# An expert stage on one Trainium2 core: low halves of the weights on GpSimd alone, gating and sparse sums in PSUM

## What is computed

```python
s1, i1 = lax.top_k(s[:, :, 0], K); s2, i2 = lax.top_k(s[:, :, 1], K)
sc, ci = lax.top_k(cand, K)                 # 16 experts for each of 8 heads
idx = e1 * PEER_NKEYS + e2; g = softmax(sc)
a = einsum('cd,chkd->chk', xc, u[ic])       # up, for the chosen rows of u
act = gelu(a) * gc
out = einsum('chk,chkd->cd', act, v[ic])    # down
```

## Time and profile before

| | us |
|---|---|
| median of 3 runs | 4909.03 (4905.62 to 4913.11) |
| the profiled execution | 4913.5 |
| its span | 4911.7 |
| busy over the whole span: TensorE, VectorE, ScalarE, GpSimd | 4389.7, 2406.8, 2512.6, 1767.7 |

### The profile page before, as it was taken

One profiled execution on the slowest core, in us unless ns is written; L12 is line 12 of the kernel. 1 busy time (PEld: TensorE's weight loads), 2 busy tenths in 40 slices (PEclk: granted clock), 3 DMA queues, 4 the chain that ended last, 5 costly groups with the idle time before them and its releaser, 6 DMA issues.

```text
span 4911.7 us, 66130 instructions
## 1 busy us (share of the span) xinstructions
PE 4389.7 (89%) x24326; PEld 2291.1 (47%) x24326; DVE 2406.8 (49%) x4548; ACT 2512.6 (51%) x3525; POOL 1767.7 (36%) x910
## 2 busy tenths in 40 slices
PE   3889999989999988997989999998897888887888
PEld 2454444544444434443444444455454554454554
DVE  4554220434334334424421022354599996796894
ACT  2457544547544445744567444364465544445444
POOL 1134433024433334443034333210342127629437
PEclk9889989999999999998899998897999999999999
DMA  3246322017322223622022322200234467768766
GB/s 145 90 152 253 105 80 82 1 50 263 128 85 85 70 70 135 252 95 69 22 73 98 100 90 82 82 31 1 75 120 133 135 185 257 252 194 281 228 199 233
DMA packets 160502, 623.60 MB, mean 127 GB/s; under 512 B 17824, under 2 KB 17952, under 8 KB 156816
## 3 DMA queue, kind: packets, MB, share of 16 engines
q1 hardware_dynamic: 123120, 483.65, 28.6%
q0 software_dynamic: 37152, 136.80, 8.8%
HBM read 618.29 MB, written 2.10 MB: 126 GB/s over the span
## 4 chain that ended last, share of the span: by engine, by line
PE 52%; DVE 19%; issue 14%; POOL 10%; ACT 3%; DMA 1%; SPq 0%; POOLq 0%; DVEq 0%; ACTq 0%
PE ps L720 13%; PE ps L722 13%; PE ps L721 13%; POOL halves L550 6%; POOL rows L606 3%; DVE halves L2550 2%; DVE rows L2512 2%; PE ps L771 2%; DVE rows L2571 1%; DVE rows L2520 1%; DVE lasting L2531 1%; DVE rows L2376 1%; PE ps L916 1%; DVE rows L2541 1%; PE ps L906 1%
## 5 line engine op out<-in xcount | busy, mean ns | idle before, releaser
L550 POOL TENSOR_TENSOR halves<-ring,halves 128x1024 f16<-128x1024 f32 x592 | 1330.2, 2248 | 2473.5 <-ACT halves L1355 2471.3
L720 PE MATMUL ps<-h,halves 128*128 128x512 f16 (+1 forms) x2912 | 1062.7, 365 | 110.5 <-POOL halves L550 72.0
L721 PE MATMUL ps<-h,halves 128*128 128x512 f16 (+1 forms) x2912 | 1061.5, 365 | 0.0
L722 PE MATMUL ps<-h,halves 128*128 128x512 f16 (+1 forms) x2912 | 1060.5, 364 | 0.0
L720 PE MATMUL ps<-rows,halves 128*128 128x512 f16 (+2 forms) x2544 | 914.8, 360 | 91.4 <-DVE rows L1948 44.0
L1352 ACT ACTIVATE ring<-ring 128x1024 f32<-128x1024 f32 x718 | 752.9, 1049 | 439.8 <-DMA ring<-wstream 436.0
L721 PE MATMUL ps<-rows,halves 128*128 128x512 f16 (+2 forms) x2544 | 913.6, 359 | 0.0
L722 PE MATMUL ps<-rows,halves 128*128 128x512 f16 (+2 forms) x2544 | 913.1, 359 | 0.0
L1355 ACT ACTIVATE halves<-ring 128x1024 f16<-128x1024 f32 x718 | 758.8, 1057 | 22.8
L720 PEld LDWEIGHTS ps<-h,halves 128*128 128x128 f16 x2912 | 287.2, 99 | 437.6 <-POOL halves L550 89.6
L722 PEld LDWEIGHTS ps<-h,halves 128*128 128x128 f16 x2912 | 287.6, 99 | 297.0 <-issue 13.5
(11 more groups left out here) (269 smaller groups left out, 5284.5 us busy)
## 6 DMA issues: line engine op xcount, KB each, us to landing
ring<-wstream SPq DMA_DIRECT2D x718, 512.0 KB
rows<-ada SPq DMA_DIRECT2D x96, 768.0 KB, 4.8
rows<-ada_first SPq DMA_DIRECT2D x24, 1024.0 KB, 5.9
x<-x_in POOLq DMA_DIRECT2D x1, 2048.0 KB, 14.0
rows<-u_rows,h POOLq DMA_INDIRECT x128
rows<-v_rows,h POOLq DMA_INDIRECT x128
out<-x SPq DMA_DIRECT2D x8, 256.0 KB, 3.9
rows<-phase_nsa SPq DMA_DIRECT2D x1, 1600.0 KB, 6.9
```

The costliest lines, as they stand in the source:

```text
L550: nc.gpsimd.tensor_tensor(halves[:, j % RING, 1, :], ring[:, j % RING, :], halves[:, j % RING, 0, :], ALU.subtract).then_inc(s_wlow, 1)
L720: nc.tensor.matmul(out_, high, act16[:, 0, :], start=first, stop=False)
L721: nc.tensor.matmul(out_, high, act16[:, 1, :], start=False, stop=False)
L722: return nc.tensor.matmul(out_, low, act16[:, 0, :], start=False, stop=last)
```

## The change

- All low halves are subtracted by GpSimd, in the same place of its queue as before; VectorE's `weights_low` is gone. ScalarE splits three slots ahead (SPLIT_AHEAD) in this stage, and first waits until TensorE has used the slot that the halves' buffer held. SP's loads of this stage wait for the low half (`s_wlow`) of the slot whose ring buffer they overwrite.
- `gated` becomes a view of PSUM banks 6 and 7: `gate` works in place where TensorE wrote. A spread then waits for the low half of the block two before (`s_actl`). Both batches of a block are spread together.
- `sparse_in` is copied by ScalarE into PSUM banks 2 and 3 before stretch 0, the steps work on that, and ScalarE copies the sum back before TensorE folds it. The up products of these stretches are left two banks, 0 and 1.
- VectorE's queue goes by blocks instead of by slots, with the choices doubled two blocks ahead.
- STEPS and LAST_STEPS are set anew: 110 steps instead of 100 in the gated stretches; the fold moves from slot 25 to 28.

```diff
--- before.py
+++ after.py
...
-STEPS = (10, 28, 56, 34, 60, 28, 40)
-LAST_STEPS = 24
+STEPS = (24, 28, 48, 28, 50, 30, 48)
+LAST_STEPS = 27
+SPLIT_AHEAD = 3
 GATHERS = 6
...
         s_step = sem("expert_rows_used")
+        s_turned = sem("sparse_input_moved")
         s_act = sem("sparse_activations")
...
-        gated = [lasting[:, i * T:(i + 1) * T].rearrange("p (e t) -> p e t", t=BLOCK) for i in range(2)]
+        gated = [ps[:, 6 + i, :].rearrange("p (t e) -> p e t", t=BLOCK) for i in range(2)]
+        sparse_ps = ps[:, 2:4, :].rearrange("p b t -> p (b t)")
         iota_h = scalars[:, 0:P // 2].bitcast(f16)
...
         def _(sp):
-            def one(n):
+            def one(n, freed):
                 if n >= RING:
-                    sp.wait_ge(s_used, n - RING + 1)
+                    sp.wait_ge(freed, n - RING + 1)
                 sp.dma_start(ring[:, n % RING, :], wstream[n]).then_inc(s_slot[n % RING], 16)
-            def stream(lo, hi):
+            def stream(lo, hi, freed=s_used):
                 whole = (hi - lo) // RING if lo >= RING else 0
...
                         for j in range(RING):
-                            sp.wait_ge(s_used, i * RING + (lo + j - RING + 1))
+                            sp.wait_ge(freed, i * RING + (lo + j - RING + 1))
                             sp.dma_start(ring[:, (lo + j) % RING, :], wstream[i * RING + (lo + j)])\
...
                 for n in range(lo, hi):
-                    one(n)
+                    one(n, freed)
...
                         late(c)
-                stream(at, end)
+                stream(at, end, s_wlow if kind == "peer" else s_used)
                 at = end
...
             first = n_slots - slots_of(stages[-1]) + 8 + E2_PART + U1_FIRST
-            lows(done, first + AHEAD)
+            lows(done, first + SPLIT_AHEAD)
             step = 0
...
                 slots = E2_PART - U1_FIRST if stretch == 0 else E2_PART
-                own = stretch in (2, 4, 6)
-                if own:
-                    pool.wait_ge(s_wlow, first + AHEAD)
                 for s in range(slots):
-                    if own and first + s + AHEAD < n_slots:
-                        weights_low(first + s + AHEAD)
+                    if first + s + SPLIT_AHEAD < n_slots:
+                        weights_low(first + s + SPLIT_AHEAD)
                     for _ in due(s, LAST_STEPS if stretch == 6 else slots, count) if s < LAST_STEPS or stretch < 6 else ():
...
-                def up(i, j, t0, n0, after=lambda k: None):
-                    pe.wait_ge(s_evac, i * 16 + (t0 + j - LIN_BANKS + 1))
+                def up(i, j, t0, n0, after=lambda k: None, banks=2):
+                    pe.wait_ge(s_evac, i * 16 + (t0 + j - banks + 1))
                     pe.wait_ge(s_wlow, i * 16 + (n0 + j + 1))
                     for k in range(C):
-                        mm = split_tile(ps[:, (t0 + j) % LIN_BANKS, 0:DENSE], (n0 + j) % RING,
+                        mm = split_tile(ps[:, (t0 + j) % banks, 0:DENSE], (n0 + j) % RING,
                                         slice(k * P, k * P + P), h16[:, k, :, SPARSE:T], k == 0, k == C - 1)
...
-                        pe.wait_ge(s_gated16, i * HALF + (b0 + j + 1))
+                        pe.wait_ge(s_actl, i * HALF + (b0 + j + 1))
                     pe.wait_ge(s_hot, i * 2 * HALF + (2 * b0 + b + 1))
...
                             for b in due(C * j + k, C * slots, count):
-                                spread(i, b, part)
+                                spread(i, 2 * b, part)
+                                spread(i, 2 * b + 1, part)
                     return after
-                def up_part():
+                def up_part(banks=2):
                     t0, n0 = seen["tile"], seen["slot"]
...
                         for j in range(16):
-                            up(i, j, t0, n0)
+                            up(i, j, t0, n0, banks=banks)
...
                         for j in range(16):
-                            down(i, j, part, n0, spread_after(i, j, gates_of, 16, 2 * HALF))
+                            down(i, j, part, n0, spread_after(i, j, gates_of, 16, HALF))
                     seen["slot"] += E2_PART
...
-                            pe.wait_ge(s_step, 2 * SPARSE)
+                            pe.wait_ge(s_turned, 2)
                             for m in range(C):
...
-                up_part()
+                up_part(LIN_BANKS)
                 for j in range(U1_FIRST):
-                    up(0, j, seen["tile"], seen["slot"])
+                    up(0, j, seen["tile"], seen["slot"], banks=LIN_BANKS)
...
                 for j in range(rest):
-                    up(0, j, seen["tile"], seen["slot"], spread_after(0, j, 0, rest, 2 * BLOCKS))
+                    up(0, j, seen["tile"], seen["slot"], spread_after(0, j, 0, rest, BLOCKS))
                 seen["tile"] += rest
...
-                def gelu(i, j, row0, t0, u0):
+                def split_high(n, loops=0, slots=0):
+                    act.wait_ge(s_used, loops * slots + (seen["used"] + n - RING + 1))
+                    weights_high(n, loops, slots)
+                def gelu(i, j, row0, t0, u0, banks=2):
                     wait_count(s_used, i * 16 + (u0 + j + 1))
                     nc.scalar.activation(acts[:, bass.ds(i * 16 + (row0 + j), 1), :].rearrange("p o t -> p (o t)"),
-                                         ps[:, (t0 + j) % LIN_BANKS, 0:DENSE], ACT.Gelu_apprx_tanh,
+                                         ps[:, (t0 + j) % banks, 0:DENSE], ACT.Gelu_apprx_tanh,
                                          scale=1.0 / W_SCALE).then_inc(s_evac, 1)
...
-                def up_part(part):
+                def up_part(part, banks=2):
                     t0, u0 = seen["tile"], seen["used"]
...
                         for j in range(16):
-                            weights_high(j + AHEAD, i, 16)
-                            gelu(i, j, E2_PART * (part % 2), t0, u0)
+                            split_high(j + SPLIT_AHEAD, i, 16)
+                            gelu(i, j, E2_PART * (part % 2), t0, u0, banks)
...
                         for j in range(16):
-                            weights_high(j + AHEAD, i, 16)
-                            for b in due(j, 16, 2 * HALF):
-                                if b % 2:
-                                    high(i, b // 2, gates_of)
+                            split_high(j + SPLIT_AHEAD, i, 16)
+                            for b in due(j, 16, HALF):
+                                high(i, b, gates_of)
...
-                up_part(0)
+                for n in range(AHEAD, SPLIT_AHEAD):
+                    split_high(n)
+                    seen["fed"] += 1
+                up_part(0, LIN_BANKS)
...
                 for j in range(U1_FIRST):
-                    weights_high(j + AHEAD)
-                    gelu(0, j, E2_PART, seen["tile"], seen["used"])
+                    split_high(j + SPLIT_AHEAD)
+                    gelu(0, j, E2_PART, seen["tile"], seen["used"], LIN_BANKS)
...
+                act.wait_ge(s_evac, seen["tile"])
+                act.wait_ge(s_picks, FOLD)
+                nc.scalar.activation(sparse_ps, sparse_in, ACT.Copy).then_inc(s_turned, 1)
                 for j in range(E2_PART - U1_FIRST):
-                    weights_high(j + AHEAD)
+                    split_high(j + SPLIT_AHEAD)
                     gelu(0, j, E2_PART + U1_FIRST, seen["tile"], seen["used"])
-                    for b in due(j, E2_PART - U1_FIRST, 2 * BLOCKS):
-                        if b % 2:
-                            high(0, b // 2, 0)
+                    for b in due(j, E2_PART - U1_FIRST, BLOCKS):
+                        high(0, b, 0)
                 seen["tile"] += E2_PART - U1_FIRST
...
                 down_part(3)
+                while seen["fed"] < n_slots:
+                    split_high(seen["fed"] - seen["used"])
+                    seen["fed"] += 1
                 seen["used"] += E2_PART
-                while seen["fed"] < n_slots:
-                    feed_one(seen["fed"])
+                act.wait_ge(s_step, 2 * SPARSE)
+                nc.scalar.activation(sparse_in, sparse_ps, ACT.Copy).then_inc(s_turned, 1)
...
-                    dve.wait_ge(s_actl, b0 + j + 1)
                     nc.vector.scalar_tensor_tensor(
-                        out=gated[j % 2], in0=ps[:, 6 + j % 2, :].rearrange("p (t e) -> p e t", t=BLOCK),
-                        scalar=1.0 / G_SCALE, in1=acts[:, lo:lo + E2_PART, j * BLOCK:(j + 1) * BLOCK],
+                        out=gated[j % 2], in0=gated[j % 2], scalar=1.0 / G_SCALE, in1=acts[:, lo:lo + E2_PART, j * BLOCK:(j + 1) * BLOCK],
                         op0=ALU.mult, op1=ALU.mult).then_inc(s_gated16, 1)
...
-                def weights_low(n):
-                    if seen["lows"] != n:
-                        dve.wait_ge(s_wlow, n)
-                    seen["lows"] = n + 1
-                    dve.wait_ge(s_whigh, n + 1)
```

(44 more changed lines are left out.)

## The result

The changed kernel took 4919.51 us in the median, the kernel before beside it 4908.84 (19 runs each): a ratio of 1.0023 with a 95% interval of 1.0016 to 1.003. It is slower by 0.2%, where 4835 and "faster" had been forecast. The profiled execution took 4918.14 us, its span 4916.4.

A forecast was written before the change was run, and what follows sets the result against it. VectorE was taken to bound the gated stretches, GpSimd stretches 2 and 4. The terms -31 - 38 - 8 + 3 sum to -74 us, giving 4835 us by the median; range 4768 to 4932, the forecast's own 4785 to 4900.

The forecast's parts named there:

- What bounds the kernel: Expert stage: VectorE bounds gated stretches, GpSimd stretches 2 and 4; a cure could give about 162 us at most.
- w: VectorE time lost per GpSimd subtraction in gated stretches (0, 1, 3, 5); taken as 0.8 us, bounds zero and 2.33.
- (b): Gated stretches: GpSimd takes 126 low halves, delaying VectorE by 0.8 us each; 665 us becomes 634, a gain of 31.
- the lock: A VectorE operation with two SBUF inputs waits for a running GpSimd subtraction; one with a PSUM input does not.
- VectorE waits for GpSimd in place of its own lows: Rival, gated stretches: subtractions hit VectorE's one-hots as a rule; 4948 us at 1.7 us each, chance 0.15.
- (c): Stretches 2 and 4: fewer gathers and faster subtractions shorten GpSimd's queue by 38 us; bounds zero and 70.
- (d): Splitting three slots ahead gains 8 us in stretches 2 and 4; earlier ring release and two up-product banks cost nothing.
- (e): Last stretch: 48 steps over 27 slots instead of 40 over 24, more gathers on GpSimd; +3 us.
- (f): ScalarE's two copies of the sparse sums and their waits, and PSUM operands on VectorE: counted as no cost.
- Held by transfers: Rival: DMA transfers hold stretches 2 and 4, so their queue gain falls away; 4877 us, chance 0.07.
- PSUM doesn't spare: Rival: sparse steps with a PSUM input still wait for subtractions, nearly cancelling the gain; 4920 us, chance 0.05.
- The lock costs nothing: Rival: under 0.3 us per subtraction, gated stretches fall to TensorE's 568 us; 4769 us in all, chance 0.20.

The follow-up runs named there:

- e1_lag1: Changed kernel with each gather one step later in GpSimd's queue (five in flight instead of six): 4844.62 us, 0.9866 of the kernel before.
- e5_lag2: Changed kernel with each gather two steps later in GpSimd's queue (four in flight instead of six): 4786.34 us, 0.9749 of the kernel before.
- e6_lag3: Changed kernel with each gather three steps later in GpSimd's queue (three in flight instead of six): 4787.42 us, 0.9749 of the kernel before.
- e9_quarter: Changed kernel, gathers two steps later, VectorE taking 8 of 32 low halves in stretches 1, 3 and 5, without waits for one-hots: 4822.29 us, 0.9822 of before.
- e2_dve_lows: Changed kernel with VectorE making the low halves of the gated stretches again: 4805.02 us, 0.9782 of the kernel before.
- e7_ahead2: Changed kernel with the split two slots ahead instead of three: 4942.18 us, 1.0062 of the kernel before.
- e8_placed: Changed kernel, gathers two steps later, VectorE taking 8 of 32 low halves in stretches 1, 3, 5, GpSimd's others waiting for the block's one-hots: 4722.44 us, 0.9618.
- e3_sums_only: Kernel before with only the sparse sums moved to PSUM, with their copies and two banks for up products: 4839.47 us, 0.9853 of the kernel before.
- e4_sums_sbuf: Changed kernel with the sparse steps working on sums in SBUF again: 5006.7 us, 1.019 of the kernel before.

## Why the prediction was wrong, point by point

**What bounds the kernel.** Right for the gated stretches: VectorE, with nothing to spare. The sum 533 + 126 w gives 782 for the kernel after (measured 782), 682 for e1_lag1 (699), 629 for e5_lag2 (642), 628 for e6_lag3 (647); with 24 low halves on VectorE and 102 w it gives 677 for e9_quarter (682), with all on VectorE 677 for e2_dve_lows (670). It is 16 short for the kernel before (665 for 681) and 69 short for e7_ahead2 (731 for 800), where TensorE waits for low halves and VectorE's gates (L2547) in turn 69.4 us for TensorE. For stretches 2 and 4 GpSimd was rightly named. Too low was "All a cure could give is thus about 162 us": e8_placed is 184 us below the kernel before beside it. A sum of waits leaves out time in which TensorE was busy but slower; its granted clock was 0.97 to 0.98 in three of the four windows of the earlier trace rows and 1.00 in stretch 1 of e8_placed. How much of the rest that makes was not measured.

**(b), the step that failed.** The prediction read the lock rightly from the earlier trace rows, its full price (2.33) and the break-even (w = 1.39). What failed is the sentence that ScalarE's order makes the subtraction come when "low and the steps are next". ScalarE did have the high half ready; the subtraction did not wait for it. It waited in GpSimd's queue behind a gather, and the gather for a sparse step, which stands just ahead of the gate. By 0.95 us of gather and 0.3 of delays the subtraction was put into the one-hots, block after block: w = 1.98 instead of 0.8, 126 x 1.18 = 149 us, which is the whole of 782 - 634 = 148. Once the gather lets go (e5_lag2), w is 0.76. That this meets the prediction's 0.8 is partly luck: over half of it comes from subtractions directly behind a gather, which the prediction named among its doubts and did not price. The order of the queue says so ("the gathers due in that slot, each waiting for the step six before"), and a row of the kernel before would have, a gather in the block of the earlier trace rows,

```profile
3963.66 1.68 POOL L606 DMA_INDIRECT rows<-u_rows,h  x1 [8.66 <-DVE h L2571]
```

which had waited 8.66 us for a step. GpSimd had been so far ahead that 96 of the 106 gathers of the gated stretches waited for a step; the subtraction put behind it was bound to inherit its phase. The rival "VectorE waits for GpSimd in place of its own lows" is what happened in the gated stretches (it gave 4948 at w = 1.7, by a chance of 0.15). Its reason, little room in a block, was not the cause of this loss: freed from the step, all 126 cost 0.76 each (e5_lag2), and e8_placed finds room for one in a block at no cost. The rival needed the phase argument; with that it would have been the likeliest.

**(c), mis-sized.** Stretches 2 and 4 gained 79.9 us, against 38 and, by (d), 8. The term took a gather's 1.72 and 1.58 us as its cost and only counted fewer of them. But the gathers, too, had been held up by the steps on SBUF: 951 ns in e3_sums_only, 1500 in e4_sums_sbuf, and after, in stretch 2:

```profile
L611 POOL DMA_INDIRECT rows<-u_rows,h x49 | 46.4, 946 | 10.1 <-issue 8.0 <-DVE h L2578 2.2
```
With 49 gathers at 0.95 and 0.2 idle, 32 subtractions at 2.14 + 0.02 GpSimd needs 56 + 69 = 125 us, just TensorE's 125. The bound of 70 for (c), "if TensorE's waits there vanish", was the right one to take; with (d)'s 8 it makes 78. (A small slip besides: in stretch 4 the term took 12.0 us of idle time, 0.20 a gather, where the earlier trace rows has 18.7 in all; it moves the sum by about 1 us.)

**(d).** The three ahead were worth 18 us in the gated stretches, beside the lock, and 4 in the last, as (e) had it; nothing in stretches 2 and 4, since those were TensorE's by then. The other parts of (d) stand: TensorE's two banks for the up products cost nothing that a row shows.

**(e).** -24.8 us in place of +3: the last stretch had the same slow gathers. **(f).** Stretch 0 begins 2.8 us later, where nothing was counted; what follows the last low half grew from 12.4 to 17.9 us. The third slot ahead is not the reason (18.2 in e7_ahead2, with two); no run separates the copy from the later fold. The PSUM operand itself cost nothing: the steps' medians are 1.21 and 1.29, gate 0.69, low 0.68.

**The other rivals.** "Held by transfers" is false: the DMA engines went from 0.83 to 0.95 of the time and from 275 to 335 GB/s. "PSUM doesn't spare" is false by e4_sums_sbuf; that its 4920 us is the time measured is luck. "The lock costs nothing" gave 4769 for the gated stretches at 568; e8_placed reached 574 once the subtraction was placed, and 4722 us, as (c) is worth more.

So a gain of 105 us in the ungated stretches met a loss of 101 in the gated ones. The forecast had -43 and -31.

## What to carry to other kernels

An engine that waits in order carries the phase of whatever stands at the head of its queue: when an operation moves behind one that always waits (here a gather with some 4 us of waiting in nearly each block), ask what releases that one, add the durations between, and look at what the other engine is doing at that moment; no average over the block says it. Where two engines lock each other out, say when, not only where: two lines of waits took 72 subtractions from about 1.4 us each to nothing. And when an operand is moved away from a shared path, look at every operation of the other engine, not only at the one that you have seen locked.

## What the runs showed of the hardware

**Gathers wait too.** GpSimd's indirect DMA took 0.95 us beside VectorE steps with one operand in PSUM, and 1.38 to 1.52 where VectorE's operations had two operands in SBUF (the earlier trace rows of the kernel before, e3_sums_only in the gated stretches, e4_sums_sbuf in a part of stretch 2). The Trainium skill (SBUF — State Buffer, Who interferes with whom) has two SBUF inputs contend with GpSimd instructions that read SBUF, and infers that making a DMA's descriptors needs the write interface, so that `tensor_tensor` does not stall a DMA issued by GpSimd. The traces differ from the second for an indirect one: 1500 ns against 946 by that one operand (e4_sums_sbuf), and 1522 in the gated stretches of e3_sums_only, where the steps are in PSUM and the operations with two SBUF inputs are `tensor_tensor`. Whether it is the gather's reading of its indices was not tried.

**The doubled copy waits as well**, for which the prediction had no row. In e9_quarter by source (shortest, median, longest ns):

```profile
L2522 DVE COPY scalars<-rows x96: 214/220/2756, 3748.0 to 4672.6; 128x128 f16<-128x128 f16 x96
```

A copy of 0.22 us takes up to 2.76, and 52 of this run's 116 us of excess stand on it. The same page has copies in two-port modes contend with GpSimd; the trace agrees as far as it goes: it shows that this copy waits, not in which mode it runs.

**The price does not follow the size of the operation that waits**: the 0.28 took 2.41 (2.13 more), the 0.68 took 2.95 (2.27 more), beside a subtraction of 2.13.
